# A state recurrence on TensorE: the two products per step that nobody reads make way for one chunk of the first pass of y

## What is computed

```python
def step(S, inp):
    r_t, w_t, k_t, v_t, kk_t, a_t = inp
    sa = jnp.einsum('bhij,bhj->bhi', S, -kk_t)
    S = (S * w_t[:, :, None, :]
         + sa[..., None] * (kk_t * a_t)[:, :, None, :]
         + v_t[..., None] * k_t[:, :, None, :])
    y_t = jnp.einsum('bhij,bhj->bhi', S, r_t)
    return S, y_t
```

## Time and profile before

| | us |
|---|---|
| median of 3 runs | 2890.9 |
| lowest, highest | 2887.91, 2892.41 |
| the profiled execution, its own time | 2876.83 |
| its span, from the first to the last instruction | 2875.2 |
| mean granted PE clock in it | 0.972 of full |

### The profile page before, as it was taken

How to read it: one execution, slowest core, us unless ns; L and a number is a source line. 1 busy time by engine, 2 the same in 40 slices (tenths; PEclk the granted TensorE clock), 3 DMA queues, 4 the chain that set the end, 5 groups by cost and what they waited for, 6 DMA issues and landing times.

```text
span 2875.2 us, 55404 instructions
## 1 busy us (share of the span) xinstructions
PE 2691.1 (94%) x21067; PEld 2284.1 (79%) x21067; DVE 1899.8 (66%) x2201; ACT 1315.2 (46%) x1414; POOL 528.4 (18%) x533
## 2 busy tenths in 40 slices
PE   7899989999898999898699999999999999999995
PEld 5797878788898999776477777777788888888884
DVE  8666747566422111344566767666789999999997
ACT  3312131131211111233456556566567777777776
POOL 5100101010000000113333233232222222222221
PEclk9999999999999999999799999999999999999998
DMA  4000000000011112232677777777699999999999
GB/s 119 15 2 17 8 10 16 2 23 2 23 44 44 44 44 66 73 101 71 220 260 274 253 266 277 261 265 259 253 396 381 381 380 381 380 381 380 380 381 340
DMA packets 143095, 537.09 MB, mean 187 GB/s; under 512 B 17842, under 2 KB 71448, under 8 KB 89478
## 3 DMA queue, kind: packets, MB, share of 16 engines
q1 hardware_dynamic: 122438, 492.78, 45.7%
q0 software_dynamic: 20544, 42.74, 6.0%
HBM read 501.04 MB, written 34.42 MB: 186 GB/s over the span
## 4 chain that ended last, share of the span: by engine, by line
PE 83%; DVE 5%; issue 4%; DMA 4%; ACT 2%; POOL 1%; POOLq 0%; SPq 0%; DVEq 0%; ACTq 0%
PE bank L880 33%; PE bank L2084 12%; PE bank L2086 12%; PE bank L2085 12%; PE bank L2093 4%; DMA raw_first<-in_w_e_down 2%; PE bank L2062 2%; PE bank L2120 1%; DVE xmix L643 1%; PE bank L1996 1%; PE bank L1998 1%; PE bank L1997 1%; PE bank L2072 1%; PE bank L2099 1%; PE bank L2154 1%
## 5 line engine op out<-in xcount | busy, mean ns | idle before, releaser
L1909 DVE TENSOR_TENSOR w_lo<-raw_first,w_hi 128x2048 fp32r<-128x2048 f32 x275 | 619.3, 2284 | 79.5 <-ACT w_hi L1683 78.2
L1683 ACT ACTIVATE w_hi<-raw_first 128x2048 fp32r<-128x2048 f32 x276 | 530.9, 1924 | 204.8 <-PE bank L2086 57.2
L2084 PE MATMUL bank<-w_hi,x_hi 128*128 128x512 f32 x1088 | 433.7, 399 | 2.1 <-ACT yo_rows L1733 2.1
L2086 PE MATMUL bank<-w_hi,x_lo 128*128 128x512 f32 x1088 | 425.4, 391 | 0.0
L2085 PE MATMUL bank<-w_lo,x_hi 128*128 128x512 f32 x1088 | 424.6, 390 | 0.0
L1909 DVE TENSOR_TENSOR w_lo<-raw_rest,w_hi 128x2048 fp32r<-128x2048 f32 x136 | 308.7, 2283 | 16.7 <-ACT w_hi L1683 16.5
L1683 ACT ACTIVATE w_hi<-raw_rest 128x2048 fp32r<-128x2048 f32 x136 | 260.7, 1918 | 118.5 <-PE bank L2120 41.5
L880 PE MATMUL bank<-xm_hi,ring_hi 128*128 128x260 f32 x896 | 261.8, 292 | 16.2 <-DVE dz L841 8.2
L880 PE MATMUL bank<-xm_lo,ring_hi 128*128 128x260 f32 x896 | 254.9, 285 | 0.0
L880 PE MATMUL bank<-xm_hi,ring_lo 128*128 128x260 f32 x896 | 254.9, 284 | 0.0
L2084 PEld LDWEIGHTS bank<-w_hi,x_hi 128*128 128x128 f32 x1088 | 204.9, 188 | 51.2 <-issue 10.3
(11 more groups left out here) (377 smaller groups left out, 4650.1 us busy)
## 6 DMA issues: line engine op xcount, KB each, us to landing
raw_first<-in_w_e_up SPq DMA_DIRECT2D x138, 1024.0 KB, 6.1
raw_first<-in_w_e_gate SPq DMA_DIRECT2D x70, 1024.0 KB, 6.4
raw_rest<-in_w_e_gate SPq DMA_DIRECT2D x70, 1024.0 KB, 4.7
raw_first<-in_w_e_down SPq DMA_DIRECT2D x68, 1024.0 KB, 6.9
raw_rest<-in_w_e_down SPq DMA_DIRECT2D x68, 1024.0 KB, 8.4
ring<-in_w_in SPq DMA_DIRECT2D x40, 512.0 KB, 3.9
hn_d<-hn SPq DMA_DIRECT2D x10, 416.0 KB
h_d<-h_all SPq DMA_DIRECT2D x10, 416.0 KB
```

The costliest lines, as they stand in the source:

```text
L1683: nc.scalar.activation(w_hi[:, j % NRING, :, :], raw_piece(j), ACT.Copy).then_inc(hi_done, 1)
L1909: nc.vector.tensor_tensor(w_lo[:, j % NRING, :, :], raw_piece(j), w_hi[:, j % NRING, :, :].bitcast(f32), ALU.subtract).then_inc(lo_done, 1)
L2084: nc.tensor.matmul(ps[:, :], hi, w_hi[:, slot, k, :], start=start and k == 0, stop=False)
L2086: ins = nc.tensor.matmul(ps[:, :], lo, w_hi[:, slot, k, :], start=False, stop=stop and k == HK - 1)
```

## The change

The first pass of y becomes a small function of the chunk, `y_of_values(c)`. Ahead of the recurrence it is called for chunk 0 alone. In step c of the recurrence, where the two unread products stood, it is called for chunk c. Products, operands, banks and the flags that open an accumulation stay as they were; the unread products are gone. No wait and no signal is added or taken away.

```diff
-            for c in range(NT):
+            def y_of_values(c):
                 for h in range(2):
                     mm(y_at(c, h), Vt[:, c, hp(h)], AT[:, 2 * c + h, 3, :], c % 4 == 0, False)
+
+            y_of_values(0)
             dve_j.done(pe, ('m', 1), j)
             for c in range(1, NT):
                 dve_j.done(pe, ('S', c - 1), j, pe_passed)
                 for h in range(2):
                     ins = mm(bank[6][hp(h), HS * (c % 2):HS * (c % 2 + 1)], mxt[hp(h), c, :], S[hp(h), c, :])
                 pe_j.mark(ins, ('s', c))
-                for h in range(2):
-                    mm(bank[2][hp(h), 0:2 * TP], mxt[hp(h), c, :], ar[hp(h), c, :, :].rearrange("p m t -> p (m t)"))
+                y_of_values(c)
             dve_j.done(pe, ('nn', 1), j)
```

## The result

| | before | after |
|---|---|---|
| median, us | 2890.8 (15 runs) | 2900.0 (15 runs) |
| lowest to highest, us (two stray runs of before left out) | 2877.9 to 2896.8 | 2893.4 to 2906.4 |
| profiled execution, its span | 2875.2 | 2900.1 |
| mean granted PE clock in it | 0.972 | 0.960 |
| ratio of the times, 95% interval | | 1.0047 (1.0035 to 1.0060) |

By the ratio the change makes the kernel slower by 0.47%, 13.6 us, with an interval of 10 to 17 us. The medians of the table are only 9.2 us apart (11.2 us with the two stray runs of before left out), so the size of the loss is known to a few us and no better. I had forecast a gain of 2.6 us; the time lies above the range. The median lies 1.6 us from rival 4, to which I had given 0.08.

The account below looks back on a forecast made before the run. PE bounds ahead of and behind the recurrence, the PE-DVE circle within. Gains 0.92 + 0 + 0.20 = 1.12 us a pass, 4.5 in four, less two clock falls of 0.95: 2890.9 to 2888.3 us; range 2882.5 to 2895.

Parts of the forecast that it names:

- rival 4: Thin recurrence: clock falls and stays down through `u` and y's passes, 3.0 us a pass; 2898.4 us, chance 0.08.
- What bounds the kernel: Recurrence and surroundings: PE bound ahead and behind, PE and DVE in turn within; a shift of its end moves all after.
- the circle with DVE: Inside the recurrence: each turn goes from PE to DVE and back, 0.80 us, and DVE releases the next step.
- Rival 2: In the recurrence: the unread products set the turn, at most 0.12 us each; 2882.6 us, chance 0.06.
- (a): Ahead of the recurrence: nine of ten chunks of y leave, so the first product with S starts 0.92 us earlier.
- (b): Inside the recurrence: y's products replace the unread ones in the steps at no cost, the turn staying 0.80 us.
- the cover: In each turn: DVE's part hides y's products, which end about 0.52 us into 0.80, leaving 0.28 us to spare.
- (c): Last step of the recurrence: `u` starts earlier behind the shorter products of y, gaining 0.20 us a pass.
- (d): Recurrence and products behind it: PE less busy, clock falls in about two of four passes, 0.95 us each.
- my own upper price: Dense products behind the recurrence: a clock fall of 3.4 us there costs 1.5 us.
- rival 3: Dense products behind the recurrence: the clock falls in every pass at 1.5 us each; 2892.4 us, chance 0.14.

Follow-up runs that it names:

- nofill: The kernel before with the unread products taken away and nothing put in their place, y still ahead of the recurrence; ratio 1.0067 (1.0042 to 1.0091).
- keep208: The changed kernel with the two unread products of 208 columns put back behind y in each step; ratio 1.0002 (0.9987 to 1.0017) against the kernel before.
- keep104: The changed kernel with the unread products put back behind y in each step, 104 columns wide; ratio 1.0011 (0.9998 to 1.0025) against the kernel before.
- work2: The changed kernel with the second pass of y also moved into the steps; ratio against the kernel before 0.9986 (0.9971 to 1.0001), run again 1.0006 (0.9993 to 1.0020).
- work3: The changed kernel with `u` also moved into the steps, second pass of y left behind the recurrence; ratio 0.9994 (0.9975 to 1.0013) against the kernel before.
- early104: The changed kernel with unread products of 104 columns put back in steps 1 to 4 alone; ratio 1.0032 (1.0014 to 1.0051) against the kernel before.

## Why the prediction was wrong, by its own steps

**What bounds the kernel.** Right for the stretch itself: once y has moved, the copy of S ahead of the recurrence, the circle with DVE within, the PE behind. The bound of the turn was shown twice, by nofill (turn 0.80 us with no product in the place of the unread ones, clock 1.00) and by keep208 (0.94 us when the PE is full). Rival 2, in which the unread products set the turn, is dead. Not borne out is the step by which I carried a gain here over to the median, that all that follows moves by as much: keep104 won 2.5 us and work2 5.6 us in the four stretches, and no median shows it clear of the scatter.

**(a) the start.** Right: 0.15 us from the copy to the product, 0.92 us won.

**(b) y in the steps costs nothing.** Right at full clock, the turn stayed 0.80 us. My account of the cover was off: y starts 0.26 us behind the product with S, not 0.13, and ends at 0.66 of 0.80 us. The loads of 104 rows behind those of 64, which I had named as not shown by any row, are one difference to the unread products that stood in that place. They aren't the whole of it: in work3 `u` stands there, whose weights take 64 rows but 104 columns, and it too starts 0.27 us behind the product with S (378.79 - 378.52). Half of the cover that I saw was there.

**(c) the last step.** Wrong in size. The early104 kernel shows it at full clock: `u` starts 0.60 us behind the last product with S, against 0.62 before, where I took 0.42. y starts 0.26 us into its turn, and `u` 0.34 us behind y instead of the 0.19 us that a chunk of y took in the old place; together these eat what its shortness brings. The term is 0.03 us, not 0.20, and the clean gain 0.95 us a pass, 3.8 us in all and not 4.5.

**(d) the clock.** This is the step that failed, in three terms. The number of falls: I took two of four, it was four of four, in both traces. The length: I took 3.4 us from the earlier trace rows, where the products behind the fall were matmuls of 104 rows; here it is 10.2 us. The price: I took 0.95 us as the middle of 0.4 and 1.5, it is 3.95 us. For dense products my price per microsecond at half clock was near, 1.5 / 3.4 = 0.44 against 3.1 us in the 6.7 us from 220.95 on, 0.46. It is the length that was three times too short, and the turn at half clock, 0.96 us where I took 0.90. In pass 0 the price of 3.95 us comes as 0.7 us from the sixth product with S to `u` (220.95 - 217.22 = 3.73 us against 3 x 0.80 + 0.60 = 3.00), 1.7 us in `u` and 1.4 us in the second pass of y (3.37 against 1.93 us); together 3.8, and its stretch is 17.05 - 13.20 = 3.85 us longer.

My reason for a possible fall was itself off in its number. I wrote that the unread products keep the PE occupied, 86% with them and about 65% without. At full clock the trace has it otherwise; five turns of after up to the fall, and five of before:

```profile
213.14:217.14 4.00, 3.31 (x40) 2.07 (x40) 1.41 (x5) 0.00 (x0) 0.00 (x0) 1.00 0.00 0
215.39:219.49 4.10, 3.44 (x42) 1.70 (x41) 1.42 (x5) 0.00 (x0) 0.00 (x0) 1.00 0.00 0
```

That is 83% against 84%, by modelled ends. The busy share hardly changed, and the clock fell in one kernel and held in the other. That the unread products hold the clock up is shown by taking them away and putting them back; by which property they do it, isn't.

I also set the row at 232.30, a stretch with the clock up at a smaller busy share, against a fall. Its matmuls are 260 columns wide and use all 128 rows; those of the recurrence are 64 and 104 wide. The row was near in its busy share alone. And I argued against rival 4 that dense products had the clock back at 205.00: that row holds for the products there. Here `u` and the second pass of y, on 64 rows, had the PE busy without a gap from 220.95 to 227.67 with the clock at 0.50 in all of it. Rival 4 had the mechanism: every pass falls, and the clock stays down through `u` and the second pass of y. Its numbers were too small, 6.8 us of half clock and 3.0 us a pass where 10.2 and 3.95 us were measured, so it gives a net loss of 7.5 us where the four stretches show 11.7. That its time lies 1.6 us from the median is in part luck; by the ratio the time is 2890.8 + 13.6 = 2904.4 us, 6 us above it. With the 10.2 us at 143.60 on record it deserved far more than 0.08.

The rule of the Trainium skill that I had set beside this ("TensorE: Matmul & The Clock Gate", "A second HAM failure mode: psum-queue depth-cycling": short idles between groups, often enough, let the clock swing) fits the changed kernel, with idle times of at most 0.6 us at a time. I had given it no weight of its own because the idle times of the old recurrence were filled. They were hardly more so: by the two rows above the PE sat idle for 0.66 of 4.10 us before, with the clock at 1.00, and for 0.69 of 4.00 us after. So the rule gives the right outcome here but doesn't tell the two kernels apart, and pass 1 of work3 fell without any idle time in its steps.

The chances followed from this. With four falls certain, the sum by my own upper price gives +1.5 us and with the real one +12.0 (4 x (3.95 - 0.95)); rival 3, the first of these, had 0.14, and nothing as dear as the second had more than 0.08.

## What to carry to other kernels

Products on TensorE whose results nobody reads can be the dearest thing to remove: before taking them out, or putting smaller ones in their place, ask what the clock does in that chain and in what follows it, and price the fall over both. A busy share read from the trace didn't warn here. Half of the filling alone was worth as much as none, while y and half of the filling together held the clock in all four passes (keep104), and filling half of the steps saved one pass in four. When the cost of a fall is read from a trace, take it from a stretch whose matmuls have the same rows and columns, and read more than one execution, for the falls elsewhere move the time of one kernel by as much as 6 us in its trace.

## What the runs showed of the hardware

- A granted clock of 0.50 lasted 10.24 us with the PE busy in all of it (217.43 to 227.67 in the changed kernel): up to 220.95 in turns of the recurrence, from there in matmuls on 64 rows. It was back at 1.00 before the first matmul on 104 rows at 227.98. In pass 1 of work3 it lasted 13.70 us with the PE busy for 13.70.
- At half clock a turn of the recurrence takes 0.96 us instead of 0.80. `u` takes 1.85 times as long (3.66 against 1.98 us), the second pass of y 1.75 times (3.37 against 1.93), its last part at full clock again.
- Products of y (weights of 104 rows and 64 columns) start 0.26 us behind the products with S (64 rows and 64 columns), and `u` (64 rows and 104 columns) 0.27 us behind them, where the unread products (64 rows and 64 columns) start 0.13 us behind them. In the steps a matmul of y lasts 252 to 303 ns at full clock, in the old place 252 to 255 ns.
- The clock fell among the steps 3.1 us (work3, pass 1) to 6.5 us (early104, pass 2) after the first product with S, with gaps of 0.47 us a turn (nofill) or with none (work3, pass 1).
